# The finest score level and the diagonal of a gated linear attention become column sums of elementwise products

## The chip, the cores and the metric
The kernel runs on one core of a Trainium2 chip. The metric is device time in microseconds (us), the median of several executions. TensorE (PE) multiplies matrices from SBUF into PSUM; VectorE (DVE) and ScalarE (ACT) work elementwise and read and write both memories; GpSimd (POOL) works elementwise in SBUF; SyncE (SP) issues the DMAs.

## The reference
Two layers, each a token mixer (HGRN2 with 8 heads in layer 0, GLA with 4 heads in layer 1) and a gated convolutional MLP, over 1024 prompt tokens and 8 streams of 16 tokens, 1152 in all, in fp32. What matters here is the recurrence of each head, with 128 key dimensions, which the reference writes as

```
S_t = diag(exp(logf_t)) S_{t-1} + k_t v_t^T,    o_t = S_t^T q_t
b = cumsum(logf)                                            # within a block
scores[t, s] = sum_d q[t,d] * k[s,d] * exp(b[t,d] - b[s,d]) # s <= t
o = scores @ v + (q * exp(b)) @ S
```

## The kernel before
Everything is fp32. Large matmuls split both operands into two float32r parts (hi, lo) and add three products (lines 657 to 659); the split of the weights is GpSimd's (lines 596, 599).

A head is one trip of `attention`, written once for each engine. Tokens lie in 9 tiles of 128, eight of the prompt and one of the streams. Scores are built by levels, `LEVELS = [64, 32, 16, 8, 4, 2, 1]`: at a level with block size m the decay between a query in the right half of a block of 2m tokens and a key in the left half is split at the middle of the block. For each level VectorE subtracts (`sub`, line 1296), ScalarE exponentiates (`level`), VectorE multiplies the left halves by k and the right halves by q (`decay`, lines 1308 and 1309), TensorE multiplies each tile by itself (line 814, plain fp32, two passes a tile), and VectorE places the wanted blocks into the score tile `a` with predicated copies (`place_scores`, line 1324). Level x uses the tile c0 (x even) or c1 (x odd), and the banks 0, 1 and 4 or 2, 3 and 5. Levels from block size 8 down (index 3 on) also have the ninth tile.

The diagonal (query and key the same token) is apart: VectorE makes q*k into c1 (line 1352), TensorE sums it over the key dimensions by nine matmuls with one column of ones (line 719, the "dots"), in the next trip, VectorE copies the nine columns out (line 1262), and when a head's output leaves PSUM, VectorE adds dot times v to it (lines 1408 and 1427).

TensorE's order within a trip is written out by hand: the first projection of the new head (`project_feature_major(0, ...)`, into banks 0 to 2, behind a wait at line 694 for all predicated copies of the head before); transposes of the previous head's decayed keys (line 716), the dots, key/value products (727), the streams' output (733, 735) and states (742); the second projection; the previous head's output (779, 781); then `MERGED` (line 322), which alternates the new head's levels with its value/gate tiles, "vg" (lines 790 to 803): level 0, vg 0, vg 1, level 1, vg 2, ... level 6, vg 7, vg 8. In the trace of a matmul inside a helper the line is 657 to 659.

After the last level VectorE prepares the previous head's state update: kh = k * exp(b_last - b) (lines 1359, 1363, 1378, in c0), qh = q * exp(b) (1367), two small copies of decays and eight for the streams (1368 to 1374). ScalarE supplies the exponentials `e` (line 1111) and that of kh (1114) and evicts the vg tiles (`take_vg`).

## Time and profile before

| | |
|---|---|
| median of 3 runs | 3102.23 us (3101.2 to 3107.43) |
| span of the profiled execution | 3104.0 us |
| TensorE busy | 2999.1 us, 97% |
| VectorE, ScalarE, GpSimd busy | 1710.3, 691.0, 1010.9 us |
| mean granted clock of TensorE | 0.985 of full speed |
| line 814, in the chain that ended last | 5% of the span |

The profiled execution is one execution of the program; only its span is listed, and it differs from the median by 1.8 us. HGRN's attention lies between about 60 and 700 us of the span, GLA's between about 1690 and 2145. Busy times of matmuls overlap, because they are pipelined, so the distance from start to start says what one costs in a row of them. "Idle before" an instruction, in square brackets, names what ended its engine's wait. The granted clock is a share of 2.4 GHz; 0.5 is the 1.2 GHz level.

### The profile page before, as it was taken

The numbers are of one execution on the slowest core, as the hardware profiler recorded it, in microseconds if no ns is written. First come the engines' busy times: TensorE is split into PE (matmuls) and PEld (weight loads), VectorE is DVE, ScalarE is ACT, GpSimd is POOL, SyncE is SP. The second block draws the span as 40 slices with busy tenths as digits, with TensorE's granted clock in tenths as the row PEclk, the third lists the DMA queues.
The fourth block names the chain that finished last, engine by engine and source line by source line (L and its number), as shares of the span: only waits on it lengthen the run. The fifth ranks groups of instructions, "written<-read, shape, count | busy, mean of one in ns | idle before, by whom it ended". The sixth has DMA issues, their size and how long they took to land.

```text
span 3104.0 us, 42637 instructions
## 1 busy us (share of the span) xinstructions
PE 2999.1 (97%) x17108; PEld 2784.4 (90%) x17108; DVE 1710.3 (55%) x2423; ACT 691.0 (22%) x1312; POOL 1010.9 (33%) x428
## 2 busy tenths in 40 slices
PE   6999999998999999999999999998999999999998
PEld 6999999997899999999997888886899999999997
DVE  3677777775654444444445565555655444444436
ACT  3333333442111100000123233233111101111112
POOL 3222222222143333333334243215034333333323
PEclk9999999999999999999999999998999999999999
DMA  3110111113111111111122012003111111111102
GB/s 121 43 42 28 38 36 36 41 46 108 35 55 42 47 41 41 41 41 41 41 67 95 26 59 70 27 29 127 35 55 42 41 47 41 41 41 47 41 28 91
DMA packets 193002, 155.82 MB, mean 50 GB/s; under 512 B 10252, under 2 KB 176204, under 8 KB 192844
## 3 DMA queue, kind: packets, MB, share of 16 engines
q1 hardware_dynamic: 192920, 154.64, 16.1%
q8 instruction: 61, 1.00, 0.1%
q14 instruction: 21, 0.17, 0.0%
HBM read 135.34 MB, written 19.28 MB: 50 GB/s over the span
## 4 chain that ended last, share of the span: by engine, by line
PE 90%; DVE 4%; ACT 2%; issue 1%; DMA 1%; POOL 1%; SPq 0%; POOLq 0%; ACTq 0%; DVEq 0%
PE bank L657 26%; PE bank L659 26%; PE bank L658 26%; PE bank L814 5%; PE bank L679 1%; PE bank L727 1%; PE bank L735 1%; PE bank L742 1%; DVE h_c L1309 1%; PE bank L719 1%; PE bank L779 1%; DVE h_c L1308 0%; PE bank L781 0%; DMA tm<-in_x_prompt 0%; DVE xt_lo L1224 0%
## 5 line engine op out<-in xcount | busy, mean ns | idle before, releaser
L596 POOL TENSOR_TENSOR ring_hi<-ring_raw,ones 128x1024 fp32r<-128x1024 f32 x197 | 440.8, 2238 | 1978.0 <-DMA ring_raw<-in_ffn_w_up 755.0
L657 PE MATMUL bank<-xt_hi,ring_hi 128*128 128x384 f32 (+1 forms) x2712 | 912.7, 337 | 9.0 <-DVE xt_lo L1224 9.0
L659 PE MATMUL bank<-xt_hi,ring_lo 128*128 128x384 f32 (+1 forms) x2712 | 908.4, 335 | 0.0
L658 PE MATMUL bank<-xt_lo,ring_hi 128*128 128x384 f32 (+1 forms) x2712 | 908.3, 335 | 0.0
L657 PEld LDWEIGHTS bank<-xt_hi,ring_hi 128*128 128x128 f32 (+1 forms) x2712 | 508.3, 187 | 17.6 <-DVE xt_lo L1224 10.6
L658 PEld LDWEIGHTS bank<-xt_lo,ring_hi 128*128 128x128 f32 (+1 forms) x2712 | 508.3, 187 | 4.7 <-issue 2.2
L659 PEld LDWEIGHTS bank<-xt_hi,ring_lo 128*128 128x128 f32 (+1 forms) x2712 | 508.2, 187 | 2.3 <-issue 0.7
L599 POOL TENSOR_TENSOR ring_lo<-ring_raw,ring_hi 128x1024 fp32r<-128x1024 f32 x197 | 504.8, 2562 | 15.5
L657 PE MATMUL bank<-ring_hi,xt_hi 128*128 128x256 f32 (+1 forms) x1152 | 402.0, 349 | 6.2 <-POOL ring_lo L599 6.2
L658 PE MATMUL bank<-ring_lo,xt_hi 128*128 128x256 f32 (+1 forms) x1152 | 391.1, 339 | 0.0
L659 PE MATMUL bank<-ring_hi,xt_lo 128*128 128x256 f32 (+1 forms) x1152 | 391.0, 339 | 0.0
L1547 DVE TENSOR_TENSOR tm<-tm,bank 128x512 f32<-128x512 f32 x360 | 247.3, 687 | 243.4 <-PE bank L659 237.3
L657 PE MATMUL bank<-ring_hi,h_hi 128*128 128x512 f32 x792 | 309.0, 390 | 0.5 <-DVE tm L1547 0.5
L659 PE MATMUL bank<-ring_hi,h_lo 128*128 128x512 f32 x792 | 308.6, 390 | 0.0
L658 PE MATMUL bank<-ring_lo,h_hi 128*128 128x512 f32 x792 | 308.5, 390 | 0.0
L1516 DVE TENSOR_SCALAR cv<-ax,params 128x1024 f32<-128x1024 f32 x88 | 53.8, 654 | 439.7 <-ACT ax L981 439.7
L981 ACT ACTIVATE ax<-bank 128x384 f32<-128x384 f32 (+2 forms) x176 | 67.5, 411 | 854.1 <-PE bank L659 854.1
L657 PEld LDWEIGHTS bank<-ring_hi,xt_hi 128*128 128x128 f32 x1152 | 222.6, 193 | 27.6 <-POOL ring_lo L599 6.5
L659 PEld LDWEIGHTS bank<-ring_hi,xt_lo 128*128 128x128 f32 x1152 | 221.4, 192 | 23.9
L658 PEld LDWEIGHTS bank<-ring_lo,xt_hi 128*128 128x128 f32 x1152 | 222.3, 193 | 21.3
L1518 DVE SCALAR_TENSOR_TENSOR cv<-ax,params,cv 128x1024 f32<-128x1024 f32 (+1 forms) x176 | 211.1, 1241 | 11.1 <-DVE cv L1518 3.9
L657 PEld LDWEIGHTS bank<-ring_hi,h_hi 128*128 128x128 f32 x792 | 148.7, 188 | 31.2 <-DVE tm L1547 0.9
(172 smaller groups left out, 3174.8 us busy)
## 6 DMA issues: line engine op xcount, KB each, us to landing
ring_raw<-in_ffn_w_up SPq DMA_DIRECT2D x88, 512.0 KB, 3.9
ring_raw<-in_ffn_w_down SPq DMA_DIRECT2D x44, 512.0 KB, 3.9
ring_raw<-in_hgrn_w_in SPq DMA_DIRECT2D x16, 512.0 KB, 4.9
tm<-in_x_prompt SPq DMA_DIRECT2D x16, 512.0 KB, 6.4
ring_raw<-in_hgrn_w_in SPq DMA_DIRECT2D x32, 256.0 KB, 3.6
ring_raw<-in_gla_w_in SPq DMA_DIRECT2D x32, 256.0 KB, 4.4
x_scratch<-tm SPq DMA_DIRECT2D x9, 512.0 KB, 2.6
tm<-x_scratch SPq DMA_DIRECT2D x9, 512.0 KB, 3.3
```

What stands on the lines that cost most here:

```text
L596: nc.gpsimd.tensor_tensor(ring_hi[slot][:, 0:width], ring_raw[slot][:, 0:width], ones[:, :].to_broadcast([P, width]), ALU.mult).then_inc(u ...
L599: nc.gpsimd.tensor_tensor(ring_lo[slot][:, 0:width], ring_raw[slot][:, 0:width], ring_hi[slot][:, 0:width].bitcast(F32), ALU.subtract).the ...
L657: nc.tensor.matmul(dst, w_hi, x_hi, start=start, stop=False)
L658: nc.tensor.matmul(dst, w_hi, x_lo, start=False, stop=False)
L659: return nc.tensor.matmul(dst, w_lo, x_hi, start=False, stop=stop)
L679: last = nc.tensor.transpose(bank[b0 + hf][:, k * P:(k + 1) * P], tm[:, t, kk * P:(kk + 1) * P], ident[:, :])
L719: last = nc.tensor.matmul(bank[7][:, t:t + 1], tile["c1"][:, t * P:(t + 1) * P], ones[:, :], start=True, stop=True)
L814: last = nc.tensor.matmul(scores(x, t), ct, ct, start=True, stop=True)
L981: return nc.scalar.activation(*a, **k)
L1516: ins = V.tensor_scalar(dst, tap(0), param(f, 0), param(f, 3), ALU.mult, ALU.add)
L1518: ins = V.scalar_tensor_tensor(dst, tap(j), param(f, j), dst, ALU.mult, ALU.add)
L1547: V.tensor_tensor(x, x, bank[6 + n][:, :], ALU.add).then_inc(AD.sem, 1)
```

## The change
The seventh level (block size 1) and the diagonal are no longer matmuls of a tile by itself. Both need one number per token, or per pair of tokens: a sum over the 128 key dimensions, which lie on the partitions. VectorE makes the products elementwise: q*k for all 1152 tokens (c1), and for the 576 pairs q of the odd token times k of the even one times the decay between the two (c0). ScalarE rounds them to float32r (`prod_hi`), VectorE subtracts to get the rest (`own_lo`, `pair_lo`, in the place of c1 and c0). TensorE multiplies by a 128x128 matrix of ones, hi and lo into one accumulation, so that every row of the result holds the sums, 512 columns at a time. Predicated copies put the pairs beside the diagonal of `a`, and with an identity mask the own products on the diagonal. The dots and their copy are gone, and the output is copied out of PSUM without the multiply-add, in pieces of 512 columns. New names: NM = 6 is the number of levels left, PAIRS = 576. In GLA `prod_hi` lies in the place of `e`.

The order and TensorE:

```diff
         MERGED = [("level", 0), ("vg", 0), ("vg", 1)]
-        for x in range(1, NL):
+        for x in range(1, NM):
             MERGED += [("level", x), ("vg", x + 1)]
-        MERGED += [("vg", t) for t in range(NL + 1, NT)]
+        MERGED += [("vg", NM + 1), ("products", 0), ("vg", NM + 2), ("products", 1)]
...
-                    for t in range(NT):
-                        last = nc.tensor.matmul(bank[7][:, t:t + 1], tile["c1"][:, t * P:(t + 1) * P], ones[:, :],
-                                                start=True, stop=True)
-                    last.then_inc(S["dots_pe"].sem, 1)
                     wait("kt", p, 3)
...
-                    wait("dots", p, 1)
...
+                        elif what == "products":
+                            hi = tile["prod_hi"]
+                            if x == 0:
+                                wait("prod_lo", i, 2)
+                                wait("pred", i, preds_after(NM - 2))
+                                parts = ((0, 0, hi[:, T:T + PROMPT // 2], tile["pair_lo"][:, 0:PROMPT // 2]),
+                                         (4, 0, hi[:, PROMPT:T], tile["own_lo"][:, PROMPT:T]),
+                                         (4, P, hi[:, T + PROMPT // 2:T + PAIRS], tile["pair_lo"][:, PROMPT // 2:PAIRS]),
+                                         (1, 0, hi[:, 0:512], tile["own_lo"][:, 0:512]))
+                            else:
+                                wait("pred", i, preds_after(NM - 1))
+                                parts = ((2, 0, hi[:, 512:PROMPT], tile["own_lo"][:, 512:PROMPT]),)
+                            for b, col, p_hi, p_lo in parts:
+                                dst = bank[b][:, col:col + p_hi.shape[1]]
+                                nc.tensor.matmul(dst, ones_r[:, :], p_hi, start=True, stop=False)
+                                last = nc.tensor.matmul(dst, ones_r[:, :], p_lo, start=False, stop=True)
+                            last.then_inc(S["prod_pe"].sem, 1)
```

ScalarE:

```diff
-                for t in range(NL - 1):
+                for t in range(NM - 1):
                     level(t + 1)
                     take_vg(t)
+                wait("pair_sub", i, 1)
+                activate(tile["c0"][:, 0:PAIRS], tile["c0"][:, 0:PAIRS], ACT.Exp, scale=K["scale"]).then_inc(S["pair_exp"].sem, 1)
+                take_vg(NM - 1)
...
+                wait("prod", i, 1)
+                activate(tile["prod_hi"][:, 0:T], tile["c1"][:, :], ACT.Copy).then_inc(S["prod_hi"].sem, 1)
+                wait("prod", i, 3)
+                activate(tile["prod_hi"][:, T:T + PAIRS], tile["c0"][:, 0:PAIRS], ACT.Copy).then_inc(S["prod_hi"].sem, 1)
+                take_vg(NM)
+                if n == "g":
+                    take_vg(NM + 1)
+                    wait("prod_pe", i, 2)
                 activate(tile["e"][:, :], tile["b"][:, :], ACT.Exp, scale=K["scale"]).then_inc(S["e"].sem, 1)
-                take_vg(NL - 1)
+                if n == "h":
+                    take_vg(NM + 1)
```

VectorE, after level 5's decay (`bs` and `bp` are b of the streams and of the prompt):

```diff
+                V.tensor_tensor(c0[:, 0, :], halves(tile["b"])[:, :, 1], halves(tile["b"])[:, :, 0], ALU.subtract
+                                ).then_inc(S["pair_sub"].sem, 1)
+                place_scores(NM - 2)
+                wait("lvl_pe", i, NM)
                 V.tensor_tensor(tile["c1"][:, :], tile["q"][:, :], tile["k"][:, :], ALU.mult).then_inc(S["prod"].sem, 1)
+                V.tensor_tensor(c0[:, 1, :], halves(tile["q"])[:, :, 1], halves(tile["k"])[:, :, 0], ALU.mult
+                                ).then_inc(S["prod"].sem, 1)
+                wait("pair_exp", i, 1)
...
+                V.tensor_tensor(c0[:, 0, :], c0[:, 0, :], c0[:, 1, :], ALU.mult).then_inc(S["prod"].sem, 1)
+                place_scores(NM - 1)
+                wait("prod_hi", i, 1)
+                V.tensor_tensor(tile["own_lo"][:, :], tile["c1"][:, :], tile["prod_hi"][:, 0:T].bitcast(F32), ALU.subtract
+                                ).then_inc(S["prod_lo"].sem, 1)
+                wait("prod_hi", i, 2)
+                V.tensor_tensor(tile["pair_lo"][:, :], c0[:, 0, :], tile["prod_hi"][:, T:T + PAIRS].bitcast(F32), ALU.subtract
+                                ).then_inc(S["prod_lo"].sem, 1)
...
+                wait("prod_pe", i, 1)
                 bp = tile["b"][:, 0:PROMPT].rearrange("p (t n) -> p t n", n=P)
                 bs = tile["b"][:, PROMPT:T].rearrange("p (s n) -> p s n", n=STREAM_T)
                 V.tensor_tensor(tile["c0"][:, PROMPT:T].rearrange("p (s n) -> p s n", n=STREAM_T), bs,
...
+                place_pairs(0, PT, bank[0][:, 0:PROMPT // 2])
+                place_pairs(PT, NT, bank[4][:, P:P + 64])
                 V.tensor_tensor(tile["c0"][:, 0:PROMPT].rearrange("p (t n) -> p t n", n=P), bp,
...
+                place_own(PT, NT, bank[4][:, 0:P])
+                place_own(0, 4, bank[1][:, :])
                 wait("e", i, 1)
                 V.tensor_tensor(tile["qh"][:, :], tile["q"][:, :], tile["e"][:, :], ALU.mult).then_inc(S["qh"].sem, 1)
...
+                wait("prod_pe", i, 2)
                 wait("kh_exp", i, 1)
                 V.tensor_tensor(tile["c0"][:, :], tile["c0"][:, :], tile["k"][:, :], ALU.mult).then_inc(S["kh"].sem, 1)
+                place_own(4, PT, bank[2][:, :])
```

The output of the prompt's eight tiles, and the two placing functions:

```diff
+                for jb in range(PT // per_job):
+                    dve.wait_ge(S["o_pe"].sem, S["o_pe"].at(p, jb + 1))
+                    V.tensor_copy(tile["v"][:, jb * per_job:(jb + 1) * per_job, :],
+                                  bank[6 + jb % 2][:, :].rearrange("p (t v) -> p t v", v=dv)).then_inc(S["o_add"].sem, per_job)
...
+                def place_pairs(t0, t1, src):
+                    nt = t1 - t0
+                    dst = tile["a"][:, t0:t1, :].rearrange("p t (g w) -> p t g w", w=2)[:, :, :, 1]
+                    msk = level_mask[:, NM * 64:NL * 64].unsqueeze(1).to_broadcast([P, nt, 64])
+                    V.copy_predicated(dst, msk, src.rearrange("p (t g) -> p t g", t=nt)).then_inc(S["pred"].sem, 1)
+
+                def place_own(t0, t1, src):
+                    nt = t1 - t0
+                    msk = own_mask[:, :].unsqueeze(1).to_broadcast([P, nt, P])
+                    V.copy_predicated(tile["a"][:, t0:t1, :], msk, src.rearrange("p (t n) -> p t n", t=nt)
+                                      ).then_inc(S["pred"].sem, 1)
```

## Rows read from the trace of the kernel before

**Rows 1.** The page's part 4: the chain that ended last, shares by engine.
```profile
PE 90%; DVE 4%; ACT 2%; issue 1%; DMA 1%; POOL 1%; SPq 0%; POOLq 0%; ACTq 0%; DVEq 0%
```
**Rows 2.** The chain in order of time, an HGRN head: start us, us, what.
```profile
263.83 2.01 PE bank L814 x18
268.71 2.01 PE bank L814 x18
...
276.48 0.18 PE bank L657
...
289.95 1.91 PE bank L719 x18
```
**Rows 3.** The same chain in a GLA head.
```profile
1870.05 2.01 PE bank L814 x18
1877.55 2.01 PE bank L814 x18
```
**Rows 4.** Timeline of ScalarE, the same HGRN head: start, us, what, [idle before].
```profile
264.19 1.18 ACT L981 ACTIVATE h_e<-h_b 128x1152 f32<-128x1152 f32 x1
...
289.44 1.25 ACT L981 ACTIVATE h_kt<-bank 128x512 f32<-128x512 f32 x3 [8.35 <-PE bank L716]
```
**Rows 5.** Timeline of VectorE at the end of that head.
```profile
265.96 1.36 DVE L1352 TENSOR_TENSOR h_c<-h_q,h_k 128x1152 f32<-128x1152 f32 x1 [0.66 <-PE bank L814]
267.24 1.46 DVE L1324 COPY_PREDICATED h_a<-level_mask,bank 128x256 f32<-128x256 uint8 x3
270.85 0.29 DVE L1359 TENSOR_TENSOR h_c<-h_b 128x128 f32<-128x128 f32 x1 [2.15 <-PE bank L814]
271.06 1.47 DVE L1324 COPY_PREDICATED h_a<-level_mask,bank 128x256 f32<-128x256 uint8 x3
272.32 1.26 DVE L1363 TENSOR_TENSOR h_c<-h_b 128x1024 f32<-128x1024 f32 x1
273.50 1.34 DVE L1367 TENSOR_TENSOR h_qh<-h_q,h_e 128x1152 f32<-128x1152 f32 x1
...
275.52 1.35 DVE L1378 TENSOR_TENSOR h_c<-h_c,h_k 128x1152 f32<-128x1152 f32 x1
```
**Rows 6.** Groups by line (busy, mean ns), VectorE, 262.3:263.3, then 271:272.6.
```profile
L1324 DVE COPY_PREDICATED h_a<-level_mask,bank 128x256 f32<-128x256 uint8 x2 | 0.8, 432 | 0.0
...
L1324 DVE COPY_PREDICATED h_a<-level_mask,bank 128x256 f32<-128x256 uint8 x2 | 1.3, 760 | 0.0
```
**Rows 7.** Timeline of GpSimd, two places in HGRN.
```profile
230.12 1.89 POOL L596 TENSOR_TENSOR ring_hi<-ring_raw,ones 128x1024 fp32r<-128x1024 f32 x1 [22.52 <-DMA ring_raw<-in_hgrn_w_in]
...
280.40 1.89 POOL L596 TENSOR_TENSOR ring_hi<-ring_raw,ones 128x1024 fp32r<-128x1024 f32 x1 [39.32 <-DMA ring_raw<-in_hgrn_w_in]
```
**Rows 8.** Timeline of VectorE around level 1, three heads.
```profile
149.00 1.22 DVE L1296 TENSOR_TENSOR h_c<-h_b 128x1024 f32<-128x1024 f32 x1
...
230.24 2.86 DVE L1296 TENSOR_TENSOR h_c<-h_b 128x1024 f32<-128x1024 f32 x1
...
312.42 2.15 DVE L1427 SCALAR_TENSOR_TENSOR h_v<-h_v,h_dot,bank 128x128 f32<-128x128 f32 x8
```
**Rows 9.** Timeline of GpSimd at the end of a GLA head.
```profile
1894.19 3.27 POOL L596 TENSOR_TENSOR ring_hi<-ring_raw,ones 128x1024 fp32r<-128x1024 f32 x1 [56.80 <-DMA ring_raw<-in_gla_w_in]
```
**Rows 10.** Timeline of TensorE: level 1 of a head, and after the last HGRN head.
```profile
325.96 3.78 PE L814 MATMUL bank<-h_c 128*128 128x128 f32 x16 [5.12 <-DVE h_c L1309]
...
684.70 1.17 PE L716 MATMUL bank<-ident,h_c 128*128 128x128 f32 x9 [0.60 <-DVE h_c L1378]
```
**Rows 11.** Windows: us, busy by engine (instructions), granted clock, DMA share, GB/s.
```profile
324.00:326.00 2.00, 0.04 (x1) 0.04 (x1) 2.00 (x2) 0.00 (x0) 1.36 (x1) 0.50 0.00 0
```
**Rows 12.** The chain in order of time, levels 1 and 2 of two heads.
```profile
241.68 3.79 PE bank L814 x16
...
249.39 1.79 PE bank L814 x16
...
332.64 1.79 PE bank L814 x16
```

More of the change, by code:

```diff
@@ L125, in build @@
         ones = place("ones", [P, 1], F32)
+        ones_r = place("ones_r", [P, P], F32R)
+        own_mask = place("own_mask", [P, P], U8)
         eps_ln = place("eps_ln", [P, 1], F32)
@@ L157, in attention_tiles @@
                 t[name] = place(f"{n}_{name}", [P, T], F32)
+            t["pair_lo"] = place(f"{n}_pair_lo", [P, PAIRS], F32R, work + 4 * T * 4)
+            t["own_lo"] = place(f"{n}_own_lo", [P, T], F32R, work + 5 * T * 4)
             kt_at = work + 2 * T * 4
@@ L169, in attention_tiles @@
             if n == "h":
+                t["prod_hi"] = place("h_prod_hi", [P, T + PAIRS], F32R)
                 t["gt"] = place("h_gt", [P, NT, dv], F32)
@@ L176, in attention_tiles @@
             else:
+                t["prod_hi"] = place("g_prod_hi", [P, T + PAIRS], F32R, at)
                 t["wgk"] = place("g_wgk", [RANK, P], F32)
@@ L182, in attention_tiles @@
             t["dec"] = place(f"{n}_dec", [P, 2 * STREAMS], F32)
-            t["dot"] = place(f"{n}_dot", [P, NT], F32)
             t["ss"] = place(f"{n}_ss", [P, NT], F32)
@@ L1260, in attention @@
                         gate(K, p)
-                    wait("dots_pe", p, 1)
-                    V.tensor_copy(tile["dot"][:, :], bank[7][:, 0:NT]).then_inc(S["dots"].sem, 1)
                     chain_tail(K, p)
@@ L1344, in attention @@
                 decay(1)
-                for x in range(2, NL):
+                for x in range(2, NM):
                     sub(x)
@@ L1407, in chain_tail @@
                 wait("odec_pe", p, 1)
-                V.scalar_tensor_tensor(tile["v"][:, PT, :], tile["v"][:, PT, :], tile["dot"][:, PT:NT], bank[7][:, 0:dv],
-                                       ALU.mult, ALU.add).then_inc(S["o_add"].sem, 1)
+                V.tensor_copy(tile["v"][:, PT, :], bank[7][:, 0:dv]).then_inc(S["o_add"].sem, 1)
                 for s in range(STREAMS):
@@ L1613, in _ @@
             V.tensor_copy(keep[:, :], keep_f32[:, :])
+            V.tensor_copy(own_mask[:, :], ident[:, :])
+            V.tensor_copy(ones_r[:, :], ones[:, :].to_broadcast([P, P]))
             h = att["h"]
```

30 lines of the change are left out of this document (15 added, 15 removed).

## Prediction

> **What bounds the kernel now.** I read the chain that ended last first: 90% of the span is TensorE [rows 1], so what counts is TensorE's own work plus every stretch in which it waits. Then the end of one middle HGRN head in that chain [rows 2]: level 5 (18 half-passes, 2.01 us) from 263.83, a value/gate tile ("vg"), level 6 from 268.71, two more vg tiles, and the next head's first projection (line 657) from 276.48. There is no gap: 268.71 - 265.84 = 2.87 us is one vg tile of 24 matmuls of 256 columns (0.120 each), and 276.48 - 270.72 = 5.76 is two. In a GLA head [rows 3] a tile is 1877.55 - 1872.06 = 5.49 us, 24 matmuls of 512 columns (0.229 each). So at the end of a head, where the change works, TensorE is the bound and VectorE and ScalarE hide beneath it.
>
> **TensorE, removed and added.** Level 6 goes: 2.01 us. The nine dots matmuls (line 719) go: 1.91 us. But the dots are cover. Next on TensorE are the key/value products of line 727, which wait for ScalarE's three copies of the transposed keys, and the last of these ends at 289.44 + 1.25 = 290.69 [rows 4], when the dots (289.95 to 291.86 in rows 2) still run. Without them TensorE waits until about 290.75 instead of going on at 291.75, so 1.0 us of the 1.91 is left. I use that for GLA too (same three copies); bounds 0.8 to 1.2.
> Added are ten fp32r matmuls with the ones as weights: in "products 0" four of 512 columns, two of 128 and two of 64, in "products 1" two of 512. At 0.229 each [rows 3], and 0.03 to 0.12 for the small ones, that is 1.1 and 0.46 us. By busy time alone a head thus loses 2.01 + 1.0 - 1.56 = 1.45 us. The rest is who waits for whom.
>
> **The wait before products 0.** VectorE makes the operands. q*k can't start before level 5 has been read (it overwrites that level's tile): line 1352 shows it at 265.96 [rows 5]. Behind it in the new order: q*k 1.36; the pair product of 576 columns 0.75 (an estimate, half of line 1352's columns and a little overhead); the product with the decay 0.75; placing level 5, 1.46 (line 1324); the low part of q*k, 1152 columns, 1.36; the low part of the pairs 0.75. Neighbours that don't wait for each other overlap by 0.08, as the starts of lines 1352 and 1324 show, so A = 6.2 us, up to 272.2. ScalarE's two roundings (1.18 us for 1152 columns in rows 4) run beneath line 1324's and the pair steps. TensorE has vg 6 and vg 7 to do until 271.4: it waits about 0.9 us in HGRN. In GLA these two tiles last 11 us: no wait.
>
> **The wait at the end of the head.** This term decides. Line 694 keeps the next head's first projection, into banks 0 to 2, until *all* predicated copies of the head are done. Before, the last of them was level 6, over at 272.5 [rows 5], long before 276.48. Now the last one (tiles 4 to 7 of the diagonal, bank 2) stands at VectorE's end, behind the product of line 1378, and the wait for products 1 stands ahead of that product. VectorE can begin only when products 0 are done and the pair operand in c0 is free: 272.3 + 1.1 + 0.3 to drain = 273.7. From there [rows 5, 6]:
> - kh's decode subtraction 0.21 to the next start (line 1359);
> - pair placement of 512 elements. Nearest rows: 256 elements at 0.43 (contiguous) and 0.76 (steps of two), so 0.7 to 1.4; I take 1.2, since its target steps by two; then 64 elements, 0.3;
> - kh's prompt subtraction (line 1363) 1.2; diagonal of the decode tile 0.25; diagonal of tiles 0 to 3, contiguous, twice 0.43 less the overlap, 0.65;
> - from the start of line 1367 to the end of line 1378, 276.87 - 273.50 = 3.37, less 0.08: 3.3;
> - the last placement, 512 contiguous elements, 0.7.
> B = 7.8 us (7.1 to 8.1), so to 281.5. The norm and gate steps of the head before queue behind that on VectorE; their next reader on TensorE is 13 us away, behind the first projection (276.48 to 289.95 in rows 2). No DMA moves: SP's loads still wait for the same projections and vg tiles. TensorE, with vg 8 and products 1 behind it (2.87 + 0.46), is idle from 276.7 to 281.6, 4.9 us. On the chain's scale the first projection starts at 281.8 instead of 276.48: +5.3 us per HGRN head (4.6 to 5.6).
> GLA: TensorE comes to the end 0.45 us sooner (2.01 off, 1.56 on). But there the exponential e now waits on ScalarE for products 1 (the rounded products lie in e's place). Behind it in ScalarE's queue are the exponential for kh, the eviction of vg 8 and the root for the norm. Chain: 0.2 drain, e 1.17, 0.1, then 3.3 and 0.7 on VectorE, 0.1: 5.5 us of waiting, so +5.1 us.
>
> **GpSimd beside it.** GpSimd splits the next vg weights about 4 us after the last vg matmul: 280.40 in HGRN [rows 7]. If it comes first, VectorE's two-input instructions suffer: line 1296 with 1024 columns took 1.22 us when it began just ahead of GpSimd, 2.86 us when GpSimd had begun 0.12 us earlier [rows 8]. The Trainium skill says why (SBUF — State Buffer, "Who interferes with whom"): the two share a port pair under an exclusive lock, and a VectorE instruction with two SBUF inputs blocks while GpSimd reads. By that rule whoever is first wins; the two rows agree.
> In HGRN line 1378 would start at 279.5, 0.9 us ahead of GpSimd: no charge. In GLA GpSimd starts 1894.19 now [rows 9] and about 0.9 us sooner afterwards (vg 8 no longer has level 6 ahead of it, only products 0), at 1893.3; line 1378 comes at about 1893.6: it loses up to one split, 1.89 us in rows 7, and I charge 1.7. GLA: +6.8 (5.1 to 9).
>
> **The clock.** A wait of 5 us has its after-effect in this trace. Where level 1 waited 5.12 us [rows 10] the granted clock stood at 0.50, the 1.2 GHz level, at the end of the wait [rows 11], and the level took 3.78 us instead of 1.79. From its start to level 2's is 332.64 - 325.96 = 6.68 us against 1.79 + 2.87 = 4.66 undisturbed: 2.0 us lost; in the head at 241.68 it is 7.71 [rows 12], 3.05 lost. The new idle ends right before the projection, so I charge 2.0 per head (0 to 3.05).
>
> **Diagonal.** Eight fused multiply-adds (2.15 us together, rows 8) become two plain copies of 512 columns, about 0.6 each by line 1352's rate: up to 1.0 us sooner ahead of level 1. ScalarE's nine squares still follow, so I take 0.2 in HGRN. In GLA TensorE doesn't wait there: 0. VectorE's dropped level-6 steps, and the two small constants made once at the start, are worth nothing: VectorE is idle beside level 6 (until line 1359), and the constants are under 1 us in all.
>
> **Sum.** HGRN, seven boundaries: 5.3 - 1.0 + 2.0 - 0.2 = 6.1, together 42.7. Last HGRN head: TensorE already waits 0.60 there for line 1378 [rows 10] and slows down afterwards; 5.3 - 0.6 - 1.0 + 0.5 - 0.2 = 4.0. GLA, three boundaries: 6.8 - 1.0 + 2.0 = 7.8, together 23.4; last head like HGRN's, 4.0. In all +74 us on a span of 3104.0: 3178. The median of the runs shown is 1.8 us below that span: 3176.
>
> **Rivals.**
> 1. *TensorE's saving prevails* (faster). If the last placement were over before TensorE needs bank 0, each head gains 1.45 us: -17, 3085; were the dots' cover not needed either, -28, 3074. For it: the 90% of rows 1. Against it: VectorE would have to finish B within vg 8 and products 1, that is 3.3 us after products 0 instead of 7.8. 6%.
> 2. *The waits come, the clock holds.* the charges of 2.0 and 0.5 go, -21: 3155. For it: the idle may fall short; against it rows 10 to 12. 15%.
> 3. *GpSimd gets in ahead of line 1378 in HGRN too.* The margin is 0.9 us, B uncertain by 0.5. One split more on seven boundaries, and a second in GLA: +13 to +19, 3192 with most of it. This is the skill's port rule in its worse order. 17%.
> 4. *The wait ahead of level 1 absorbs a part.* TensorE waits 5.12 us there anyway. If that wait hung on GpSimd's or the DMA's own pace, 3 us per HGRN boundary would go: 3155. Against it: in the chain it starts from the end of the second projection, which moves along. 8%.
>
> My forecast has 52%, and 2% is left for no change to measure. About 0.2% (6 us) is what can be told from no change here. Slower: 0.92; same 0.02; faster 0.06. The range runs from rival 2 or 4 with the short B (0.7 on twelve heads, 8) and no charge for GpSimd (5), 3142, to all of rival 3 (19) with the long clock loss (1.05 on ten boundaries, 11), 3206.
>
> **What would show it.** In the profile afterwards: line 657's first projection waiting about 5 us in eleven heads for VectorE's predicated copy; the granted clock at 0.5 right after; products 0 late by about 1 us in HGRN and on time in GLA; line 727 waiting about 1 us for ScalarE; TensorE's busy share below 97% though it has fewer matmuls. I am wrong if that first projection follows products 1 without a gap.

## The result, and the profile after

| | before | changed |
|---|---|---|
| median | 3104.8 us (4 runs: the three listed above and one more, 3101.2 to 3108.2) | 3175.8 us (4 runs, 3173.2 to 3181.4) |
| span of the profiled execution | 3104.0 us | 3171.8 us |
| TensorE busy | 2999.1 us, 97% | 3002.7 us, 95% |
| mean granted clock | 0.985 | 0.976 |

The changed kernel is slower: ratio 1.0233, 95% interval 1.0218 to 1.0248, some 71 us. The forecast was 3176.

TensorE has fewer instructions (16796 instead of 17108) and is busy for as long as before, because part of its work ran at half the clock. Its waits, from the view that groups them (line waited at, released by: us in total, times, longest), are the first thing to read. These seven rows are the largest that are new; rows that both kernels have grew by at most 1.4 us, and the waits before the levels (line 836, 814 before) fell from 34.2 to 25.9:

```profile
PE bank L666 <- DVE h_a L1417: 31.6, 7, 4.5
PE bank L666 <- DVE g_a L1417: 16.0, 3, 5.3
PE bank L732 <- ACT h_kt L1003: 6.2, 8, 0.8
PE bank L725 <- DVE g_a L1417: 5.4, 1, 5.4
PE bank L823 <- DVE h_pair_lo L1405: 4.9, 8, 0.6
PE bank L725 <- DVE h_a L1417: 4.6, 1, 4.6
PE bank L732 <- ACT g_kt L1003: 3.1, 4, 0.8
```

The first two rows are the boundary wait: the next head's first projection (now line 666) waits for the last placement of the diagonal (line 1417) in front of seven HGRN and three GLA heads. The rows of line 725 are the same wait in the two last heads, where no projection follows and the transposes wait. Line 732 (key/value products, 727 before) waits for ScalarE's copies, which the dots had covered; line 823 is products 0. Together 72 us, but TensorE also got rid of work, so the sum of the waits is not the loss. For that a head is laid against a head.

The kernel before was profiled a second time (further down), and in that execution no head was disturbed by GpSimd. One HGRN head of it, timeline of TensorE (start us, us, what, [idle before it and what ended that]):

```profile
289.09 1.14 PE L716 MATMUL bank<-ident,h_c 128*128 128x128 f32 x9
313.43 1.95 PE L814 MATMUL bank<-h_c 128*128 128x128 f32 x16
324.39 2.05 PE L814 MATMUL bank<-h_c 128*128 128x128 f32 x16 [3.26 <-DVE h_c L1309]
330.27 2.05 PE L814 MATMUL bank<-h_c 128*128 128x128 f32 x16 [0.96 <-DVE h_c L1309]
344.81 2.17 PE L814 MATMUL bank<-h_c 128*128 128x128 f32 x18
357.46 0.34 PE L657 MATMUL bank<-xt_hi,ring_hi 128*128 128x384 f32 x1
369.95 1.14 PE L716 MATMUL bank<-ident,h_c 128*128 128x128 f32 x9
```

The same head of the changed kernel:

```profile
307.54 1.15 PE L725 MATMUL bank<-ident,h_c 128*128 128x128 f32 x9
309.48 2.05 PE L732 MATMUL bank<-h_v,h_kt 128*128 128x128 f32 x16 [0.80 <-ACT h_kt L1003]
330.93 1.95 PE L836 MATMUL bank<-h_c 128*128 128x128 f32 x16
341.16 2.78 PE L836 MATMUL bank<-h_c 128*128 128x128 f32 x16 [2.54 <-DVE h_c L1341]
347.46 1.95 PE L836 MATMUL bank<-h_c 128*128 128x128 f32 x16
361.90 2.17 PE L836 MATMUL bank<-h_c 128*128 128x128 f32 x18
370.45 0.50 PE L823 MATMUL bank<-h_prod_hi,ones_r 128*128 128x512 f32 x1 [0.63 <-DVE h_pair_lo L1405]
379.95 0.69 PE L666 MATMUL bank<-xt_hi,ring_hi 128*128 128x384 f32 x1 [4.53 <-DVE h_a L1417]
394.05 1.15 PE L725 MATMUL bank<-ident,h_c 128*128 128x128 f32 x9
```

The distances from start to start give the account (us):

| from, to | before | changed | difference | forecast |
|---|---|---|---|---|
| transposes, level 0 | 24.34 | 23.39 | -0.95 | -1.0 (dots) |
| level 0, level 1 | 10.96 | 10.23 | -0.73 | -0.2 (diagonal) |
| level 1, level 2 | 5.88 | 6.30 | +0.42 | 0 |
| level 2, level 5 | 14.54 | 14.44 | -0.10 | 0 |
| level 5, next first projection | 12.65 | 18.05 | +5.40 | +5.3 |
| first projection, transposes | 12.49 | 14.10 | +1.61 | +2.0 (clock) |
| sum | 80.86 | 86.51 | +5.65 | +6.1 |

The +0.42 belongs to the pair of heads shown: level 1 ran at a granted clock of 1.00 in the first and 0.70 in the second. In the five other middle heads of that profile of before, level 1 to level 2 takes 6.2 to 6.4 us, and over all six the difference is 0.1. In every second head the last distance is 15.12 us (292.42 to 307.54), that is +2.63. Over six periods the mean is 87.05 us against 81.13 (126.64 to 613.41 in the second profile of before): +5.9. In GLA it is 116.10 against 110.24: again +5.9.

The slow projection is the granted clock. Windows right after the wait (from 205.77, the projection of the head before; us, TensorE busy, granted clock, DMA share, GB/s):

```profile
205.80:207.80 2.00, 2.00 (x6) 0.50 0.08 22
207.80:211.80 4.00, 4.00 (x21) 0.83 0.00 0
```

After 4.52 us of idle the clock stands at 0.50, the 1.2 GHz level, as in [rows 11], and is still 0.83 in the mean of the 4 us after that. In the heads with 15.12 us it is lower there: 0.57 from 294.45 to 298.45.

What holds line 666 back is VectorE's queue at the end of a head. Its timeline, one HGRN head:

```profile
189.95 1.36 DVE L1393 TENSOR_TENSOR h_c<-h_q,h_k 128x1152 f32<-128x1152 f32 x1 [3.24 <-PE bank L836]
...
195.41 0.75 DVE L1405 TENSOR_TENSOR h_pair_lo<-h_c,h_prod_hi 128x576 fp32r<-128x576 f32 x1
198.04 0.29 DVE L1424 TENSOR_TENSOR h_c<-h_b 128x128 f32<-128x128 f32 x1 [1.88 <-PE bank L824]
198.25 1.47 DVE L1412 COPY_PREDICATED h_a<-level_mask,bank 128x512 f32<-128x512 uint8 x2
...
200.89 0.92 DVE L1417 COPY_PREDICATED h_a<-own_mask,bank 128x128 f32<-128x128 uint8 x2
...
203.72 1.35 DVE L1448 TENSOR_TENSOR h_c<-h_c,h_k 128x1152 f32<-128x1152 f32 x1
204.99 0.72 DVE L1417 COPY_PREDICATED h_a<-own_mask,bank 128x512 f32<-128x512 uint8 x1
```

From q*k to the end of the low parts: 196.16 - 189.95 = 6.21 us (A, forecast 6.2). From the decode subtraction to the end of the last placement: 205.71 - 198.04 = 7.67 (B, forecast 7.8). TensorE starts 0.06 us later, at 205.77.

### The profile page after: what moved, and what is told of

It is laid out like the page before. It is cut to its first block, busy times and chain, and to the rows that moved or that the text cites. A ratio compares the mean times of both kernels' runs of the same rounds, so it can differ in the third digit from the quotient of the medians.

```text
span 3171.8 us, 42076 instructions
## 1 busy us (share of the span) xinstructions
PE 3002.7 (95%) x16796; PEld 2777.8 (88%) x16796; DVE 1756.5 (55%) x2397; ACT 702.7 (22%) x1324; POOL 1023.1 (32%) x428
## 4 chain that ended last, share of the span: by engine, by line
PE 85%; DVE 6%; ACT 2%; issue 2%; POOL 1%; DMA 1%; SPq 0%; POOLq 0%; ACTq 0%; DVEq 0%
PE bank L666 25%; PE bank L668 25%; PE bank L667 25%; PE bank L836 4%; PE bank L732 1%; PE bank L688 1%; PE bank L739 1%; PE bank L783 1%; PE bank L746 1%; PE bank L785 1%; DVE h_c L1341 0%; ACT h_junk L1003 0%; DVE h_a L1417 0%; DVE h_a L1412 0%; DVE h_a L1356 0%
## 5 line engine op out<-in xcount | busy, mean ns | idle before, releaser
L666 PE MATMUL bank<-xt_hi,ring_hi 128*128 128x384 f32 (+1 forms) x2712 | 925.0, 341 | 56.5 <-DVE h_a L1417 31.6
L667 PE MATMUL bank<-xt_lo,ring_hi 128*128 128x384 f32 (+1 forms) x2712 | 917.9, 338 | 0.0
L666 PEld LDWEIGHTS bank<-xt_hi,ring_hi 128*128 128x128 f32 (+1 forms) x2712 | 515.3, 190 | 69.4 <-DVE h_a L1417 34.6
L608 POOL TENSOR_TENSOR ring_lo<-ring_raw,ring_hi 128x1024 fp32r<-128x1024 f32 x197 | 515.2, 2615 | 15.5
L667 PEld LDWEIGHTS bank<-xt_lo,ring_hi 128*128 128x128 f32 (+1 forms) x2712 | 515.8, 190 | 4.6 <-issue 2.2
L668 PEld LDWEIGHTS bank<-xt_hi,ring_lo 128*128 128x128 f32 (+1 forms) x2712 | 514.8, 190 | 2.3 <-issue 0.7
L668 PEld LDWEIGHTS bank<-ring_hi,h_lo 128*128 128x128 f32 x792 | 148.7, 188 | 30.9
```

What stands on the lines that cost most here:

```text
L608: nc.gpsimd.tensor_tensor(ring_lo[slot][:, 0:width], ring_raw[slot][:, 0:width], ring_hi[slot][:, 0:width].bitcast(F32), ALU.subtract).the ...
L666: nc.tensor.matmul(dst, w_hi, x_hi, start=start, stop=False)
L667: nc.tensor.matmul(dst, w_hi, x_lo, start=False, stop=False)
L668: return nc.tensor.matmul(dst, w_lo, x_hi, start=False, stop=stop)
```

## The experiments

All but two start from the changed kernel; "the changed kernel" in an expectation is that one, at 3175.8 us.

**The wait, split by bank.**

```diff
-                    wait("pred", i - 1, S["pred"].per)
-                    project_feature_major(0, (0, 1, 2), ...)
+                    placed = preds_after(NM - 1)
+                    project_feature_major(0, (0, 1, 2), ...,
+                                          before=lambda c: wait("pred", i - 1, placed + (2, 4, 5)[c]))
```

> The changed kernel (median 3175.8 us; the kernel before 3104.8), with one wait of TensorE split: the next head's first projection waits bank by bank for the placements that still read that bank, not for all five. Theory (the loss is this one wait and the half clock behind it): the boundary waits of 4.5 us (eight HGRN heads) and 5.3 us (four GLA heads) go, and with them the slow stretch behind them (2.15 and 1.6 us at the ten middle boundaries). Sum: 8 x 4.5 + 4 x 5.3 + 7 x 2.15 + 3 x 1.6 = 77 us at most. Of that the GpSimd and VectorE work behind it may give a little back, so I expect 3098 to 3112 and a granted clock near 0.985. Rival (the wait only stands for VectorE being late): TensorE then stops a little later, at the transposes for the product with the keys, and the time stays above 3150.

Measured: 3108.1 us (10 runs, 3101.1 to 3112.0), ratio to before 1.0005 (0.9994 to 1.0016). Of the 71 us some 68 go with this wait. The HGRN period is 79.9 or 80.3 us, below the 81.1 of before. Line 666 no longer appears with a placement. The waits for ScalarE (6.2 us in HGRN) and before products 0 (4.9) are as they were, and the two last heads still wait:

```profile
PE bank L726 <- DVE g_a L1418: 5.4, 1, 5.4
...
PE bank L726 <- DVE h_a L1418: 4.6, 1, 4.6
```

The rival (the stall only moves on to the transposes) is right for the two last heads, 4.6 and 5.4 us, which have no projection to hide VectorE's work, and wrong for the ten others.

**The idle filled.** Eighteen fp32r matmuls of 512 columns that nobody reads, behind products 1.

```diff
+                            if x == 1:
+                                for _ in range(18):
+                                    nc.tensor.matmul(bank[3][:, :], ones_r[:, :], xt_hi[:, 0, 0:512], start=True, stop=True)
```

> The changed kernel with 18 matmuls of 512 columns that nobody reads, put behind products 1 of every head, into bank 3, where TensorE would otherwise stand idle for 4.5 to 5.3 us (18 x 0.229 = 4.1 us). They are work added, and the wait itself stays. Theory (half of what a boundary costs beyond its wait is the granted clock that falls in the idle): the first projection behind them runs at the full clock, from its start to the transposes 12.5 us instead of 14.1 to 15.2, so 7 x 2.15 + 3 x 1.6 = 20 us are gained, 3176 to about 3156. Rival (the projection is slow for another reason, for example its operands or GpSimd beside it): no gain, 3176, or more if the filler runs past the wait.

Measured: 3170.5 us, only 5 less. But where the theory speaks, it holds: the projection behind the filler takes 12.59 us, with the full clock from its first window,

```profile
204.25 0.45 PE L666 MATMUL bank<-xt_hi,ring_hi 128*128 128x384 f32 x1 [0.43 <-DVE h_a L1420]
...
216.84 1.14 PE L725 MATMUL bank<-ident,h_c 128*128 128x128 f32 x9
```

and the window at its start

```profile
204.30:206.30 2.00, 2.00 (x12) 1.00 0.04 12
```

and all six HGRN periods between the first seven heads are 85.0 to 85.1 us instead of 87.05. GLA shows it in one period (114.7 instead of 116.1) and not in the next (116.2). There the projection is fast too (12.6 us), but the head behind it loses 1.6 us before level 0, where for a stretch the granted clock is 0.72 with TensorE busy throughout (1974 to 1980); in the head before, the same stretch ran at 1.00. The last head loses as much at the same place, and GLA as a whole gains nothing (334.6 us against 334.3). Why the clock falls there stays open; the same stretch stands at 0.72 in two runs below that have no filler (the output copies taken apart, VectorE made late), so it can't be put down to the filler. The rest of the gain went into the feed-forward part of layer 0, where six pauses ended by nothing the profile shows add up to 12.3 us. The next run asked about them.

**The idle filled with few instructions.** The same, with five plain fp32 matmuls of 512 columns.

> As the filler run with 18 short matmuls, but the idle before the first projection is filled by 5 fp32 matmuls of 512 columns (some 0.86 us each, 4.3 us in all), so that hardly any instruction is added. The run with 18 showed the period of a middle HGRN head at 85.05 us instead of 87.05, which is the theory's 2 us per boundary, but gave it back in six pauses of TensorE (12.3 us together, in the loop of the feed-forward part, released by nothing the profile shows). Theory (those pauses come with the added code or by chance, and have nothing to do with the clock): period 85.05 again, fewer pauses, total 3176 - 14 - 3 = 3157 to 3163. Rival (what is kept in the boundary is paid later, because a busier TensorE is granted less clock or stalls more in the feed-forward part): pauses as before and the total stays near 3170.

Measured: 3168.1 us (3158.9 to 3173.7). The period is 85.0 again, so the clock theory stands a second time. The pauses stayed, five of them, with hardly any code added; so the expected total of 3157 to 3163 was wrong, and with it the guess that the longer code made them. The total and the pauses are as the rival had them; that the gain is paid back because TensorE is busier isn't shown by that, since pauses come without a filler too, as the next runs show.

**What the pauses are.** The two kernels were profiled once more, unchanged.

> The kernel before once more, unchanged, for its profile alone. Open is whether the pauses of about 2 us in the feed-forward parts (none in the profiles of the two kernels, one to six in those of the experiments) belong to a kernel's code or to the single execution, and whether the first projections start at 43.2 us each time. If to the execution: the stages of attention repeat within 0.5 us, and the feed-forward parts (897.6 us each) differ by multiples of some 2 us. If to the code: both parts read 897.6 again.

> The changed kernel once more, unchanged, for its profile alone. Pauses by execution: the HGRN heads read 593.6 us and the GLA heads 334.3 again, within 0.5, and the feed-forward parts (898.5 and 897.7) differ by multiples of some 2 us; the first transposes lie within 2 us of 133.4. Pauses by code: the feed-forward parts repeat too.

Measured: 3101.8 and 3174.9 us. The second profile of the changed kernel has one pause where the first had none:

```profile
1373.77 0.44 PE L666 MATMUL bank<-xt_hi,ring_hi 128*128 128x384 f32 x1 [2.25 <-issue]
```

So the same code has them in one execution and not in the other. That the code has no part in how often they come isn't shown: the two profiles with fillers have three and five fetches, the eleven others none to two. They come only where the trip of the feed-forward loop starts again, and each goes with 9 more packets of the instruction queue. The row of that queue in part 3 of the page (packets, MB, share) reads 61 packets in the three profiles without a pause (both of before, the first of the changed kernel), and in the second profile of the changed kernel, with one,

```profile
q8 instruction: 70, 1.15, 0.1%
```

79 with the split wait (two pauses), and with the short filler, which has five,

```profile
q8 instruction: 106, 1.74, 0.2%
```

61 + 9 = 70, 61 + 2 x 9 = 79, 61 + 5 x 9 = 106: now and then TensorE's code is fetched again at the loop's branch, a pause of about 2.2 us each time. (The filler with 18 matmuls shows 88, that is three, each with a pause on either side of a group of matmuls.) The Trainium skill (Runtime: NRT & Kernel Launch, "Instruction fetch mechanics") says that a taken branch whose target isn't in the window held forces a fetch before the engine goes on; the rows agree, and add that here it happens in some trips and not in others.

The pause isn't always the whole cost. Behind the one at 1373.77 TensorE ran for about 6 us at a granted clock of 0.76, then 0.69 (columns as above):

```profile
1375.80:1379.80 4.00, 4.00 (x19) 0.69 0.00 0
```

The feed-forward part of layer 0, from its first projection to the transposes of its tails (line 974), takes 764.3 us in the three profiles without a fetch and 768.3 to 768.4 in the seven that have one there, so such a fetch costs about 4 us. With the split wait the clock stayed at 1.00 behind both pauses, and the part takes 769.2, 4.9 more for two; the long filler's three fetches, with their six pauses, cost 17.0.

One expectation missed: before's HGRN part didn't repeat within 0.5 us. It reads 561.4 and 555.2, without a pause in either; the runs on level 1 below explain most of it. Stages are therefore compared, not totals, where a few microseconds count:

| us | before, profiles 1 and 2 | changed, 1 and 2 |
|---|---|---|
| to the first transposes | 123.3, 126.6 | 133.4, 131.8 |
| HGRN, first to last transposes | 561.4, 555.2 | 593.6, 593.7 |
| to GLA's first transposes | 1107.9, 1107.4 | 1117.7, 1121.0 |
| GLA, first to last transposes | 319.2, 319.1 | 334.3, 334.3 |
| to the end | 992.3, 991.6 | 992.8, 992.2 |

**The output copies taken apart.**

```diff
-                    V.tensor_copy(tile["v"][:, jb * per_job:(jb + 1) * per_job, :], ...).then_inc(S["o_add"].sem, per_job)
+                    for x in range(per_job):
+                        V.tensor_copy(tile["v"][:, jb * per_job + x, :],
+                                      bank[6 + jb % 2][:, x * dv:(x + 1) * dv]).then_inc(S["o_add"].sem, 1)
```

> The changed kernel with its two copies of 512 output columns (four in GLA) taken apart into eight copies of one tile each, as many instructions as the fused multiply-adds of the kernel before. Theory (the two large copies bring VectorE ahead of GpSimd before level 1, so that its wait is 2.54 us in every HGRN head where the kernel before showed 3.3 or 5.1): level 1 is again late by 3.3 or 5.1 us in at least some heads, and the time rises by 5 to 12 us, to 3181 to 3188. Rival (what I predicted: 0.2 us per head): at most 2 us more, and level 1's wait stays within 0.3 of 2.54.

Measured: 3175.5 us, no change; level 1 waits 2.66 us, HGRN takes 593.3. The theory as it was put falls: it isn't the size of the copies. The trace shows what it is instead: eight copies take 1.81 us (the multiply-adds 2.15, [rows 8]), and in the six middle heads the subtraction for level 1 still starts ahead of GpSimd, by 0.3 to 0.6 us. In the second profile of before the two meet like this (VectorE, then GpSimd):

```profile
233.57 1.22 DVE L1296 TENSOR_TENSOR h_c<-h_b 128x1024 f32<-128x1024 f32 x1
234.71 1.35 DVE L1447 TENSOR_TENSOR tm<-tm,h_v 128x1152 f32 x1
...
233.61 4.20 POOL L596 TENSOR_TENSOR ring_hi<-ring_raw,ones 128x1024 fp32r<-128x1024 f32 x1 [23.11 <-DMA ring_raw<-in_hgrn_w_in]
```

and in the changed kernel:

```profile
244.19 1.22 DVE L1328 TENSOR_TENSOR h_c<-h_b 128x1024 f32<-128x1024 f32 x1
245.32 3.05 DVE L1515 TENSOR_TENSOR tm<-tm,h_v 128x1152 f32 x1
...
244.58 2.57 POOL L605 TENSOR_TENSOR ring_hi<-ring_raw,ones 128x1024 fp32r<-128x1024 f32 x1 [27.79 <-DMA ring_raw<-in_hgrn_w_in]
```

Before, the order is a matter of a tenth of a microsecond: 0.04 us ahead of GpSimd, as here, the subtraction takes 1.22 us and level 1 waits 3.26; 0.12 behind it [rows 7, 8], it takes 2.86 and level 1 waits about 5.1 [rows 10]. (Within 0.1 us the recorded starts don't tell who is first: other undisturbed heads of before have VectorE up to 0.07 us behind.) In the changed kernel VectorE is 0.39 us ahead in that head, 0.4 to 0.5 in the others, and level 1 waits 2.54 us in all six middle heads. Between 3.26 and 2.54 the order isn't turned, since the subtraction takes 1.22 us in both; what differs is the instruction behind it. Before, the product of line 1447 gets through as well and GpSimd's split takes 4.20 us; in the changed kernel GpSimd comes in between, the split takes 2.57 and the product (now line 1515) 3.05. The product with k that level 1 needs (lines 1308 and 1340) then takes 2.59 us before and 1.53 after.

**VectorE made late.** One copy of 512 columns more (0.69 us, into a tile nobody reads) ahead of the second output copy, in HGRN.

```diff
+                    if n == "h" and jb == PT // per_job - 1:
+                        V.tensor_copy(tile["prod_hi"][:, 0:512], bank[6 + jb % 2][:, :])
```

> The changed kernel with one more copy of 512 columns (0.69 us, into a tile that nobody reads) ahead of the second output copy on VectorE in HGRN heads. The trace of the changed kernel has the subtraction for level 1 start at 244.19, 0.39 us ahead of GpSimd's split (244.58), and take 1.22 us; the kernel before has it 0.09 us behind a split, and it takes 2.89. Theory (the gain of about 0.65 to 1.5 us per head before level 1 is the order of these two): the subtraction now starts 0.2 to 0.3 us behind the split and takes 2.9 us or more; the wait before level 1 rises from 2.54 to 4 to 5.1 us in the middle HGRN heads, and with 7 of them the time rises by 10 to 18 us, to 3186 to 3194. Rival (the copies' own length is all): the wait rises by 0.7 at most, 3176 to 3181.

Measured: 3193.2 us (3188.4 to 3198.6), 17 more than the changed kernel, for eight copies of 0.69 us. The order has turned:

```profile
246.51 2.85 DVE L1328 TENSOR_TENSOR h_c<-h_b 128x1024 f32<-128x1024 f32 x1
...
246.39 1.90 POOL L605 TENSOR_TENSOR ring_hi<-ring_raw,ones 128x1024 fp32r<-128x1024 f32 x1 [27.78 <-DMA ring_raw<-in_hgrn_w_in]
...
257.95 3.79 PE L836 MATMUL bank<-h_c 128*128 128x128 f32 x16 [5.16 <-DVE h_c L1341]
```

Level 1 waits 5.1 to 5.2 us in four of the six middle heads, whose periods are 90.1 to 90.7 us, and 3.06 in two, with 86.9; in those two the subtraction starts 0.01 us behind GpSimd and still takes 1.22. So whether level 1 waits about 3 or about 5 us hangs on which of these two instructions comes first. In the profile HGRN takes 607.1 us, 13.5 more. GLA takes 2.7 more (337.0), though this edit leaves it alone; it did so in the run before, too, and 1.6 of it lie in the stretch of lower clock named above.

**The last placement first.** The placement of tiles 4 to 7 ahead of the product with the keys.

```diff
+                place_own(4, PT, bank[2][:, :])
                 wait("kh_exp", i, 1)
                 V.tensor_tensor(tile["c0"][:, :], tile["c0"][:, :], tile["k"][:, :], ALU.mult).then_inc(S["kh"].sem, 1)
-                place_own(4, PT, bank[2][:, :])
```

> The changed kernel with the last placement (512 columns of the diagonal, 0.72 us) moved ahead of the product of exponential and keys (1.35 us) on VectorE; the wait for products 1 that stood between is taken a few instructions earlier, where it is over. Theory (the length of the boundary wait is VectorE's queue): the wait falls by 1.3 us to 3.2 and 4.0, the half clock behind it stays for the most part, and the time falls by 12 x 1.3 = 15 us, to about 3160; if the shorter idle keeps the clock up, by up to 20 more. In GLA the product with the keys now starts 0.4 us after GpSimd's split instead of 0.3 before it: by the port rule it takes 2.5 to 3.2 us instead of 1.35, off TensorE's path, since the transposes come 12 us later. Rival (GpSimd's lock also holds up predicated copies): the placement itself takes over 1.5 us in GLA and the four GLA boundaries gain nothing, so 3166.

Measured: 3162.0 us, 13.8 less. The waits are 3.3 and 4.0. GLA shows the port as expected, and that the placement isn't touched by it:

```profile
1931.46 0.72 DVE L1417 COPY_PREDICATED g_a<-own_mask,bank 128x512 f32<-128x512 uint8 x1
1932.07 2.80 DVE L1449 TENSOR_TENSOR g_c<-g_c,g_k 128x1152 f32<-128x1152 f32 x1
...
1931.77 1.89 POOL L605 TENSOR_TENSOR ring_hi<-ring_raw,ones 128x1024 fp32r<-128x1024 f32 x1 [56.32 <-DMA ring_raw<-in_gla_w_in]
```

The product starts 0.30 us behind the split and takes 2.80 us instead of 1.35. In the last GLA head, where TensorE waits for that product, the swap costs: 6.8 us instead of 5.4.

**The dots alone.** The kernel before without its dots; the diagonal is left out of the output.

```diff
-                    for t in range(NT):
-                        last = nc.tensor.matmul(bank[7][:, t:t + 1], tile["c1"][:, t * P:(t + 1) * P], ones[:, :], ...)
-                    last.then_inc(S["dots_pe"].sem, 1)
...
-                    V.tensor_copy(tile["dot"][:, :], bank[7][:, 0:NT]).then_inc(S["dots"].sem, 1)
+                    V.memset(tile["dot"][:, :], 0.0).then_inc(S["dots"].sem, 1)
```

> The kernel before, without the nine dots matmuls of each head (1.91 us): the sums are set to zero, so the diagonal is left out of the output. Theory (the dots are cover for ScalarE's copies of the transposed keys, and 0.95 us of them is left): the transposes-to-key-products distance falls from 2.90 to 1.95 us, 12 heads x 0.95 = 11 us less, about 3094; where the earlier operands also bring VectorE ahead of GpSimd before level 1, up to 1.9 us more in half of the HGRN heads, 3086. Rival (the busy time is what counts): 12 x 1.91 = 23 us less, 3082, with the key products 0.99 us after the transposes.

Measured: 3109.6 us (11 runs, 3099.4 to 3115.7), ratio to before 1.0014 (1.0003 to 1.0025): no gain at all in the total, against both theories. The local part of the first one holds,

```profile
447.66 1.15 PE L716 MATMUL bank<-ident,h_c 128*128 128x128 f32 x9
449.60 2.05 PE L723 MATMUL bank<-h_v,h_kt 128*128 128x128 f32 x16 [0.80 <-ACT h_kt L977]
```

1.94 us from transposes to key products, as expected. GLA takes 316.4 us (319.1 before) and undisturbed HGRN heads 80.1 to 80.2 (81.1), so some 0.95 per head. In HGRN the gain is spent: three of the heads come behind GpSimd or behind the clock's fall (81.3 to 82.7 us), and the eight take 554.6 (555.2 in the second profile of before). Two pauses make up 4.1 us of the profile, and some 6 with the slower clock behind the first. Why the median stands 5 us above that of before over eleven runs, these don't settle; more frequent pauses would do it, and the profile is of one execution.

**A version put together from the findings.** The split wait, and: the decode product ahead of the key products, as cover for ScalarE's copies; level 5 placed behind the low parts; the subtraction for the keys' exponential in VectorE's idle before products 0 (the low part of the pairs moves to another tile's place).

> The changed kernel with its waits rearranged: the first projection waits bank by bank (as in the run with the split wait, 3108 us); the decode product moves ahead of the key products, so that it covers ScalarE's copies; level 5 is placed behind the low parts, which products 0 wait for; the subtractions for the keys' exponential run in VectorE's idle 1.9 us before products 0 are done (the low part of the pairs lies in the place of another tile for that). The theory by terms against 3108: 0.8 us less in each of 12 heads at the key products, 0.6 less in eight HGRN heads at products 0, about 1.2 less in each of the two last heads, which wait for the product with the keys: -17, 3091, and up to 5 more if two pauses in the feed-forward part don't recur: 3085 to 3095, that is 0.3 to 0.6% less than the kernel before. Rival (these waits are covered, or turn into later ones at level 1): 3100 to 3110.

Measured: 3110.5 us, above the 3085 to 3095 expected and just past the rival's 3110, and the two layers tell opposite tales. HGRN takes 537.4 us, 17.8 under the second profile of before, as the terms said. GLA takes 335.6 (319.1). There two placements had been put behind the product that waits for `e`, and so VectorE's small copies met GpSimd:

```profile
1880.43 6.34 DVE L1445 COPY g_qz<-g_qh 128x16 f32<-128x16 f32 x8
...
1880.41 1.94 POOL L605 TENSOR_TENSOR ring_hi<-ring_raw,ones 128x1024 fp32r<-128x1024 f32 x1 [56.19 <-DMA ring_raw<-in_gla_w_in]
...
2116.93 2.15 PE L726 MATMUL bank<-ident,g_c 128*128 128x128 f32 x9 [11.85 <-DVE g_a L1418]
```

Eight copies of 16 columns that take 0.70 us alone took 6.34 once GpSimd had begun 0.02 us before them, and 4.6 to 6.3 in the three other GLA heads. The boundary wait is back in GLA (3.5 to 5.6 us, 12.6 in three heads), and the last head waited 11.85 us.

**The same, mended for GLA.** GLA keeps its order of placements, and its products 1 come ahead of the ninth value tile.

```diff
+                    if n == "g":
+                        order = order[:-2] + [order[-1], order[-2]]
```

> The rearranged version again, with its GLA part mended. In the run before it the eight HGRN heads took 537.4 us from first to last transposes (561.4 in the kernel before), as worked out, but GLA lost 15 us: the placements behind the exponential pushed VectorE's small copies behind GpSimd's split, and eight copies that take 0.71 us took 6.34. Now GLA keeps its order of placements, and both groups of products come ahead of the ninth value tile there, so that the exponential no longer waits for the end of the head. Expected: HGRN 537 again; GLA from first to last transposes 320.3 (split wait alone) - 3 x 0.8 - about 3.4 in the last head = 314 to 315; the sum of the stages 3078 with no pause in the feed-forward parts, with two to four of 2.2 us a median of 3080 to 3090, 0.5 to 0.8% less than the kernel before. Rival (GpSimd's splits hit VectorE's copies in GLA whatever the order): GLA stays at 320 or more, 3086 to 3096.

Measured: 3080.5 us (5 runs, 3076.1 to 3081.5), ratio to before 0.9915 (0.9902 to 0.9929): faster than both kernels. HGRN takes 538.1 us and GLA 315.2, close to the expected 537 and 314 to 315. What each of the rearrangements gives by itself wasn't run. What is left of the wait for placements, in the last head of each layer:

```profile
PE bank L726 <- DVE h_a L1420: 3.5, 1, 3.5
PE bank L726 <- DVE g_a L1420: 2.1, 1, 2.1
```

## Why the prediction was right, and where its terms were off

- *The deciding step held in its parts.* A 6.21 us (forecast 6.2), B 7.67 (7.8), the boundary wait 4.53 (4.9), GLA's 5.32 (5.5), products 0 late by 0.63 in HGRN (0.9) and on time in GLA. From level 5 to the projection 18.05 us; the chain put it at 281.8 - 263.83 = 17.97. The split wait, which leaves all the work in place and removes only this, takes the loss away: shown, not only argued.
- *The clock.* 1.6 and 2.6 us in turn in HGRN, 1.6 in GLA; forecast 2.0. Both fillers give it back in HGRN, so rival 2 (the clock holds) was wrong and the charge right. In GLA the projection behind the filler ran at the full clock too, but two heads lost 1.6 us elsewhere. That the 2.0 came so close is partly luck: the 6.68 us from level 1 to level 2 that it was read from were set against 1.79 + 2.87 = 4.66, and no middle head of before shows that distance. Undisturbed, it is 5.9 to 6.4, because TensorE waits 0.96 us for VectorE there or runs at the lower clock. What does hold is the level's own length, 3.78 us instead of 1.79.
- *The dots as cover.* 0.95 us per head (1.0).
- *The diagonal was sized wrong.* Forecast 0.2 us in HGRN. It took the copies' own length and ScalarE's squares, and left out what stands in rows that it had used for another term: the meeting of line 1296 and GpSimd in [rows 7, 8]. The wait at level 1 falls from 5.1 to 2.54 against a disturbed head, because the order turns. Against an undisturbed one it falls from 3.26, with VectorE first in both: VectorE comes some 0.4 us sooner beside GpSimd, which then gets in behind the subtraction. Of these 0.72 us the size of the copies is 0.12 (2.66 with eight small ones). The first profile of before had three heads longer than the rest by 1 to 3 us (two with GpSimd first, one where the granted clock was 0.50 from level 1 on and level 2 came 7.5 us later); against it HGRN grew by 32.2 us, against the second, with none, by 38.5.
- *GpSimd's charge in GLA was zero instead of 1.7.* It came 0.30 us behind the product with the keys (1944.97 against 1944.67), 0.15 and 0.10 behind it at the two other boundaries, not ahead. A difference of a few tenths of a microsecond between two chains, each known to about half a microsecond, should have been a chance and not a full charge. The mechanism is real: the swapped placement turned the order, and the product took 2.80 us. Rival 3, the same in HGRN, did not come: GpSimd started at 205.00, 1.3 us behind that product (203.72).
- *Rival 4* (level 1's wait absorbs a part): no, as the account's second row shows; it shrank by itself.
- *The sum.* Forecast +74 on the span. Measured +67.8 between the first profiles and +73.1 between the second (3173.0 - 3099.9). By boundaries, against the undisturbed profile: HGRN 5.9 instead of 6.1, its last head 3.0 instead of 4.0, GLA 5.9 instead of 7.8, its last head 3.4 instead of 4.0: 7 x 5.9 + 3.0 + 3 x 5.9 + 3.4 = 65. So the terms were 9 too high in all, most of it GpSimd's charge (5.1) and the two last heads (1.6). The other 8 us were in no term of the forecast. In the second profile 4.1 of them are the fetch of code (a pause of 2.3 and the slower clock behind it); 1.5 come between the last HGRN transposes and the feed-forward part (157.4 us instead of 156.0); and 1.4 before level 0 of the first GLA head, where TensorE waits 7.5 us for GpSimd's split instead of 6.2 and the clock stays low for longer behind it (0.53 from 1763.6 to 1767.6, where the second profile of before has 0.89 from 1714.6 to 1718.6). About 1 us is left untraced. That the median came out at the forecast to a microsecond is partly luck.
- *The signs.* The first projection was to wait in eleven heads; it waits in ten, seven and three, as the sum itself has it. The last head of each layer has no projection behind it and waits at the transposes.

## What to carry to other kernels

Work taken off the bounding engine is gained only if whatever replaces it on another engine is over before the bounding engine's next instruction asks for it: before moving a reduction from matmuls to elementwise work, write down the queue behind the last new instruction and who waits for its end, and give each bank its own wait instead of one for all. Where two engines meet within a few tenths of a microsecond on a shared port, treat the order as a chance, and look for an order that keeps them apart by more. Compare stages rather than totals when single executions differ by more than the effect.

## What the runs showed of the hardware that was not expected

- VectorE's copies of 16 columns from SBUF to SBUF are held by GpSimd, but not all of them: of the eight at 1880.43 three took 1.87, 2.39 and 1.87 us, beside GpSimd instructions of 1.94, 2.46 and 1.91, and the five others 0.16 each; alone they take 0.17. Each copy that is caught waits for the end of the GpSimd instruction beside it, and a few get through between two of these. The Trainium skill (SBUF — State Buffer, "Who interferes with whom") counts copies among the instructions that can take the shared port; the trace agrees.
- Predicated copies from PSUM with a mask in SBUF are not held: 512 contiguous elements took 0.72 us with GpSimd's split beginning in the middle of them (1931.46 and 1931.77), and 0.72 when it ran already (1887.96, the run before the mended one).
- TensorE's code is fetched again in some trips of the feed-forward loop: 9 packets and a pause of about 2.2 us each, none to five per execution. A single one cost the feed-forward part of layer 0 about 4 us in seven profiles, where the granted clock fell behind the pause, and two cost 4.9 where it didn't.
- With TensorE busy throughout, the granted clock was 0.72 in a stretch of 6 us before level 0 of a GLA head: in two heads of each filler run, and in one head of each of two runs without a filler. No row gives a reason.
